# One transformer layer on one core: first feed-forward layer in 512-column matmuls, masked products of a block in one group

## The chip, the core and the metric

The kernel runs on one core of a Trainium2 chip. The metric is the device time of one execution in microseconds (us). TensorE (PE) multiplies matrices and writes to PSUM, which has eight banks of 512 float32 values a partition; VectorE (DVE) and ScalarE (ACT) read PSUM and do elementwise work; GpSimd (POOL) has little to do here; SyncE (SP) issues the loads.

## The reference

One layer with 256 tokens and a width of 1024:

```
h = RMSNorm(x); P = h @ W_in
mixer A: RWKV-7 recurrence, 8 heads x 64 (delta-rule state), + bonus sum(r k r_k) v
mixer B: causal attention, 8 heads x 64;   mixer C: causal pooling
x = x + (sum of sigmoid gates * branch projections) @ W_out
h2 = RMSNorm(x)
x = x + square(relu(h2 @ w_ff1)) @ w_ff2        w_ff1: 1024 x 4096
```

All is float32. The recurrence is computed in blocks of 128 tokens: masked products of two token-wise operands give small matrices, a triangular system is solved by levels, and four steps of 64 tokens carry the state.

## The kernel before

**Precision.** Each float32 factor is held as a high part and a rest: w_hi and w_lo of the weights, h_hi and h_lo of the activations, r_hi and r_lo of the feed-forward's hidden values. A product is three matmuls (`mm3`, lines 497 to 499): high by high, high by rest, rest by high, added up in PSUM.

**Pieces and slots.** The dense work is a list of 69 units (`UNITS`), one for each slot t. A slot uses two weight pieces of 512 KB, v = 2t and 2t + 1, and has four quarters p = 0 to 3; a place in the program is written (t, p). For every quarter each engine runs the dense part (`part`) and then what else is put there (`extra`): of the mixers on TensorE, and their copies on ScalarE and VectorE. SyncE loads a piece into one of three stages once VectorE has finished the piece three before (`lo_done`); ScalarE rounds it to w_hi (L900), VectorE subtracts to w_lo (L1142). The ring of split pieces has six places: ScalarE may write piece v when TensorE has used piece v - 6 (`used`). The splits run about five pieces ahead of TensorE. Engines follow their own program strictly in order, so an instruction that waits holds up what stands behind it.

**Banks.** `plan_turns` deals the banks out in the order of the program, and `room` makes TensorE wait until the bank's former content was copied out (`drained`). In the slots spoken of here banks 0 to 3 belong to the dense units and 4 to 7 go around in a ring.

**Slots 7 to 11.** At (7, 3) TensorE transposes v into two banks, 5 and 6; ScalarE copies these to zz (L961). The masked products of block c are computed in two groups g of two head pairs, each with 32 small matmuls (L626, L629) into two banks; `PROD_AT` puts the groups at (8, 0), (8, 2), (9, 0) and (9, 2). The bonus, two float32 matmuls of 512 columns from `att` (L706), stands at (8, 1); the profile lists each as two passes. VectorE masks the products (L1246) and multiplies the bonus into v (L1237). X0 (L722), transposes of the first solution, follows at (9, 1) and (10, 1); Y, the first level of the solution (L743), at (11, 0).

**Feed-forward, slots 37 to 68.** A first-layer unit ("ff1", i) computes 256 of the 4096 hidden columns, as two column tiles of 128 by 8 k, with weights as the stationary operand and h2 (256 tokens) as the moving one: 48 matmuls of 256 columns into one bank. ScalarE takes Relu out of PSUM (L1097) and squares it into r_hi (L1101); VectorE computes the square (L1428) and the rest r_lo (L1146). A second-layer unit ("ff2", i) multiplies these: 24 matmuls of 512 columns into banks 0 to 3, where they add up to the end. The order is ff1 0, ff1 1, ff2 0, ff1 2, ff2 1 and so on, so that ff2 i starts two slots after the end of ff1 i, in the case of the first and the last unit one slot after. The transposes of x for h2 (L881) stand at (36, 1) and (37, 0), their drains at L1051 and L1386.

Of the kernel before, what the change touches and what calls it, by code (L numbers as in the profile page):

```python
# [76 lines left out]
PROD_AT = {(8, 0): (0, 0), (8, 2): (0, 1), (9, 0): (1, 0), (9, 2): (1, 1)}  # L77
# [44 lines left out]
def plan_turns():  # L122


    turn, count, signalled, ring = {}, [0] * 8, [0] * 8, [4, 5, 6, 7]

    def use(name, bank=None, dense=False):
        if bank is None:
            bank = ring[0]
            ring.append(ring.pop(0))  # L130
        turn[name] = (bank, count[bank], signalled[bank])
        count[bank] += 1
        signalled[bank] += not dense

    for i in range(4):
        use(("x", i))
    for t, u in enumerate(UNITS):
        if t == S_HEAD:
            ring.insert(0, 3)
        if t == S_BR:  # L140
            ring.remove(3)
        for p in range(4):
            if p == 0:
                if u[0] == "feat":
                    use(("unit", t), FEAT_BANK[t], dense=True)
                elif u[0] == "tok" and u[2] == 0 and u[1] >= GATES_AT:
                    g = (u[1] - GATES_AT) // 512
                    for tt in range(TT):
                        use(("tok", u[1], tt), (2 * g + tt + 2) % 3, dense=tt == 1)
                elif u[0] == "tok" and u[2] == 0:  # L150
                    b = 0 if u[1] == N_RWKV else 2
                    use(("tok", u[1], 0), b + 1)
                    use(("tok", u[1], 1), b, dense=True)
                elif u[0] == "branch":
                    b = 2 * ((t - S_BR) % 2)
                    use(("unit", t, 0), b)
                    use(("unit", t, 1), b + 1, dense=True)
# [23 lines left out]
def pe_uses(t, p):  # L181
# [57 lines left out]
    if h2_place(t, p) is not None:  # L239
        out += [(("h2", 2 * h2_place(t, p) + i),) for i in range(2)]  # L240
# [3 lines left out]
def dense_ends():  # L244

    ends = {}
    for t, u in enumerate(UNITS):
# [9 lines left out]
        if u[0] == "ff1":  # L257
            ends[("ff", u[1])] = 2 * t + 2
# [6 lines left out]
def build_layer(nc: bass.Bass, x, w_in, w_up, w0, a_up, g_up, pool_w, w_branch, w_out, w_ff1, w_ff2, vecs, consts, out):  # L265
    turn = plan_turns()
    ctx = ExitStack()
    with ctx:
# [10 lines left out]
        h_hi = sb("h_hi", [P, KD, T], F32R)  # L279
        h_lo = sb("h_lo", [P, KD, T], F32R)  # L280
# [146 lines left out]
        f_hi, f_ready = sem("f_hi"), sem("f_ready")  # L427
# [67 lines left out]
        def _(pe):  # L495
# [37 lines left out]
            def part(t, p):  # L533
# [6 lines left out]
                if u[0] in ("feat", "ff1"):  # L540
                    name = ("unit", t) if u[0] == "feat" else ("ff", u[1])
# [5 lines left out]
                    for kk in range(4):  # L547
                        k = 4 * (p // 2) + kk
                        if k % 2 == 0 and u == ("ff1", 0) and i == 0:
                            copied(pe, ("h2", k // 2))  # L550
# [90 lines left out]
            def extra(t, p):  # L641
# [60 lines left out]
                if (t, p) == (8, 1):  # L702
# [12 lines left out]
                if (t, p) in PROD_AT:  # L715
                    products(*PROD_AT[t, p])
# [177 lines left out]
        def _(act):  # L894
# [22 lines left out]
            def extra(t, p):  # L917
# [128 lines left out]
                if h2_place(t, p) is not None:  # L1046
                    for i in (2 * h2_place(t, p), 2 * h2_place(t, p) + 1):
# [4 lines left out]
                        ins.then_inc(h2_hi, 1)  # L1052
                if (t, p) == (S_FF, 1):
# [7 lines left out]
            def finish(t):  # L1061
# [30 lines left out]
                elif u[0] == "ff1":  # L1092
                    i = u[1]
                    if i >= 2:
                        act.wait_ge(f_ready, i - 1)
                    o = take(act, ("ff", i))
                    nc.scalar.activation(ffs[i % 2], o[:], ACT.Relu).then_inc(drained_of(("ff", i)), 1)  # L1097
                    copied(act, ("ff", i))
                    if i >= 2:
                        act.wait_ge(used, 2 * (UNITS.index(("ff2", i - 2)) + 1))  # L1100
                    nc.scalar.activation(r_hi[:, 2 * (i % 2):2 * (i % 2) + 2], ffs[i % 2].rearrange("p (k t) -> p k t", k=2),  # L1101
                                         ACT.Square).then_inc(f_hi, 1)
# [27 lines left out]
        def _(dve):  # L1130
# [49 lines left out]
            def extra(t, p):  # L1180
# [51 lines left out]
                if (t, p) == (8, 1):  # L1232
# [6 lines left out]
                if (t, p) in PROD_AT:  # L1239
                    c, g = PROD_AT[t, p]  # L1240
                    if g == 0:
                        dve.wait_ge(mask_in, 16)
                    for e in range(2):
# [136 lines left out]
                if h2_place(t, p) is not None:  # L1380
                    for i in (2 * h2_place(t, p), 2 * h2_place(t, p) + 1):
# [6 lines left out]
                        ins.then_inc(drained_of(("h2", i)), 1)  # L1388
                if (t, p) == (S_FF, 3):
# [4 lines left out]
            def finish(t):  # L1394
# [30 lines left out]
                elif u[0] == "ff1":  # L1425
                    i = u[1]
                    copied(dve, ("ff", i))
                    link(dve.tensor_tensor(fsq[i % 2], ffs[i % 2], ffs[i % 2], ALU.mult))  # L1428
                    dve.wait_ge(f_hi, i + 1)
                    b = 2 * (i % 2)  # L1430
                    rest(r_lo[:, b:b + 2], fsq[i % 2].rearrange("p (k t) -> p k t", k=2), r_hi[:, b:b + 2])\
                        .then_inc(f_ready, 1)
# [139 lines left out]
```

## Time and profile before

| | us |
|---|---|
| median of 3 runs | 467.64 (467.38 to 467.68) |
| the profiled execution | 467.01 |
| span of its instructions | 465.2 |
| TensorE busy | 459.6 (99%) |
| VectorE, ScalarE busy | 295.0 (63%), 245.8 (53%) |
| granted TensorE clock, mean | 1.00 |

Busy time of TensorE counts the whole time of pipelined matmuls, which overlap: a matmul of 512 columns is listed with 0.39 us and the next one starts 0.23 us after it. So the distance between starts tells its pace, and a gap in busy time shows only part of a wait.

### The profile page before, as it was taken

The page shows a single profiled execution, that of the slowest core. Times are in us where ns is not written, and L with a number is a line of the kernel's source. Part 1 is how long each engine was busy: PE and PEld are TensorE (multiplying, and loading weights), DVE is VectorE, ACT ScalarE, POOL GpSimd, SP SyncE. Part 2 cuts the span into 40 slices and gives each one's busy share as a digit, 9 for nine tenths or more (in the row PEclk, how much of TensorE's full clock was granted, in tenths as well). Part 3 has the DMA queues.
Part 4 walks back from the last instruction along what each step waited for, and adds up shares of the span by engine and source line. Part 5 has one row for each costly group of instructions (what it writes and reads, how often), then busy time and mean ns, then how long its engine had stood idle before and what let it go on. Part 6 is the DMA issues. An engine that isn't in the chain of part 4 may idle for free.

```text
span 465.2 us, 8736 instructions
## 1 busy us (share of the span) xinstructions
PE 459.6 (99%) x3660; PEld 397.7 (85%) x3660; DVE 295.0 (63%) x405; ACT 245.8 (53%) x370; POOL 33.1 (7%) x41
## 2 busy tenths in 40 slices
PE   8999999999999999999999999999999999999997
PEld 4999986788977778788888889999999999999995
DVE  4675998674564766766778758655555555555542
ACT  5597655646555456566543538444444444444430
POOL 2000100021670001002000000000000000000000
PEclk9999999999999999999999999999999999999999
DMA  7776635533424435445656564655556656565602
GB/s 235 235 231 217 220 96 177 151 122 93 145 87 136 118 110 142 130 159 171 189 185 184 175 193 143 209 184 184 184 189 194 197 184 182 185 182 190 204 10 90
DMA packets 48694, 76.91 MB, mean 165 GB/s; under 512 B 2576, under 2 KB 28944, under 8 KB 48656
## 3 DMA queue, kind: packets, MB, share of 16 engines
q1 hardware_dynamic: 48656, 76.36, 53.1%
q8 instruction: 29, 0.48, 0.4%
q14 instruction: 9, 0.07, 0.0%
HBM read 75.30 MB, written 1.05 MB: 164 GB/s over the span
## 4 chain that ended last, share of the span: by engine, by line
PE 90%; DVE 3%; ACT 2%; DMA 2%; issue 1%; POOL 1%; DVEq 0%; ACTq 0%
PE bank L497 26%; PE bank L498 25%; PE bank L499 25%; DMA stage<-in_w_in 2%; PE bank L606 1%; PE bank L762 1%; PE bank L743 1%; DVE w_lo L1142 1%; PE bank L638 1%; ACT w_hi L900 1%; POOL small L1472 1%; DVE xs L1458 1%; PE bank L626 1%; PE bank L829 1%; PE bank L793 1%
## 5 line engine op out<-in xcount | busy, mean ns | idle before, releaser
L1142 DVE TENSOR_TENSOR w_lo<-stage,w_hi 128x1024 fp32r<-128x1024 f32 x138 | 167.9, 1225 | 89.1 <-ACT w_hi L900 89.1
L900 ACT CAST w_hi<-stage 128x1024 fp32r<-128x1024 f32 x138 | 144.5, 1052 | 109.5 <-PE bank L499 88.6
L497 PE MATMUL bank<-h_hi,w_hi 128*128 128x256 f32 x384 | 109.8, 286 | 0.3 <-DVE h_lo L1386 0.3
L498 PE MATMUL bank<-h_lo,w_hi 128*128 128x256 f32 x384 | 108.6, 283 | 0.0
L499 PE MATMUL bank<-h_hi,w_lo 128*128 128x256 f32 x384 | 108.6, 283 | 0.0
L497 PEld LDWEIGHTS bank<-h_hi,w_hi 128*128 128x128 f32 x384 | 73.6, 192 | 1.6 <-issue 0.8
L498 PEld LDWEIGHTS bank<-h_lo,w_hi 128*128 128x128 f32 x384 | 73.6, 192 | 0.6
L499 PEld LDWEIGHTS bank<-h_hi,w_lo 128*128 128x128 f32 x384 | 73.6, 192 | 0.0
L497 PE MATMUL bank<-w_hi,h_hi 128*128 128x512 f32 x144 | 60.4, 420 | 0.0
L497 PE MATMUL bank<-w_hi,r_hi 128*128 128x512 f32 x144 | 56.4, 392 | 0.0
L499 PE MATMUL bank<-w_hi,h_lo 128*128 128x512 f32 x144 | 56.4, 391 | 0.0
L498 PE MATMUL bank<-w_lo,h_hi 128*128 128x512 f32 x144 | 56.4, 391 | 0.0
L498 PE MATMUL bank<-w_lo,r_hi 128*128 128x512 f32 x144 | 56.2, 390 | 0.0
L499 PE MATMUL bank<-w_hi,r_lo 128*128 128x512 f32 x144 | 56.0, 389 | 0.0
L497 PEld LDWEIGHTS bank<-w_hi,h_hi 128*128 128x128 f32 x144 | 27.0, 188 | 7.7 <-issue 2.4
L499 PEld LDWEIGHTS bank<-w_hi,h_lo 128*128 128x128 f32 x144 | 27.0, 188 | 6.1
L499 PEld LDWEIGHTS bank<-w_hi,r_lo 128*128 128x128 f32 x144 | 27.0, 188 | 5.8
L497 PEld LDWEIGHTS bank<-w_hi,r_hi 128*128 128x128 f32 x144 | 27.1, 188 | 5.2
L498 PEld LDWEIGHTS bank<-w_lo,r_hi 128*128 128x128 f32 x144 | 27.1, 188 | 4.9
L498 PEld LDWEIGHTS bank<-w_lo,h_hi 128*128 128x128 f32 x144 | 27.1, 188 | 4.7 <-issue 0.2
L1472 POOL TENSOR_TENSOR small<-small 128x8 f32<-128x8 f32 (+2 forms) x9 | 15.0, 1676 | 173.7 <-DVE small L1320 69.1
L1097 ACT ACTIVATE mat<-bank 128x512 f32<-128x512 f32 x16 | 9.6, 599 | 30.5 <-PE bank L499 30.5
(231 smaller groups left out, 541.9 us busy)
## 6 DMA issues: line engine op xcount, KB each, us to landing
stage<-in_w_ff SPq DMA_DIRECT2D x64, 512.0 KB, 3.8
stage<-in_w_in SPq DMA_DIRECT2D x54, 512.0 KB, 3.8
stage<-in_w_branch SPq DMA_DIRECT2D x12, 512.0 KB, 4.5
stage<-in_w_out SPq DMA_DIRECT2D x8, 512.0 KB, 4.1
xs<-in_x SPq DMA_DIRECT2D x2, 512.0 KB, 3.9
out<-xs SPq DMA_DIRECT2D x4, 256.0 KB, 2.1
cst<-in_consts SPq DMA_DIRECT2D x1, 608.0 KB, 6.6
att<-in_w SPq DMA_DIRECT2D x1, 256.0 KB, 5.9
```

The source lines that it names most:

```text
L497: pe.matmul(o, lh, rh, start=first, stop=False)
L498: pe.matmul(o, lh, rl, start=False, stop=False)
L499: return pe.matmul(o, ll, rh, start=False, stop=last)
L606: pe.matmul(banks[3][:], flat[:, 0:P], flat[:, 0:512], start=True, stop=True)
L626: ins = pe.matmul(o[halves[e], P * i:P * i + P], bk[c][halves[e], j, s, 0:HD], ar[c][halves[e], j, :, HD * s:HD * s + HD], start=True, sto ...
L638: ins = pe.transpose(o[:, P * j:P * j + P], x_c[:, c, j].rearrange("p s n -> p (s n)"), ident)
L743: ins = pe.matmul(both[e][halves[s], HD * i:HD * i + HD], gm[c][halves[e], j, s, e, 0:HD], x_c[halves[e], c, j, s], start=True, stop=True)
L762: ins = pe.matmul(both[s][halves[e], HD * i:HD * i + HD], left, right, start=True, stop=True)
L900: nc.scalar.copy(w_hi[:, v % RING], stage[:, v % STAGES]).then_inc(hi_done, 1)
L1097: nc.scalar.activation(ffs[i % 2], o[:], ACT.Relu).then_inc(drained_of(("ff", i)), 1)
L1142: dve.tensor_tensor(w_lo[:, v % RING], stage[:, v % STAGES], w_hi[:, v % RING].bitcast(F32), ALU.subtract)\
L1472: pool.tensor_tensor(ap, ap, half.to_broadcast(shape), ALU.pow).then_inc(done, 1)
```

## The change

In the first feed-forward layer h_hi and h_lo now lie in one tensor, `h_two` (128 x 2 x 8 x 256). High by high and high by rest have the same stationary weights, and are one matmul of 512 columns: its first 256 results are w_hi x h_hi, the others w_hi x h_lo. The third, w_lo x h_hi, has 256 columns and is added to the second half. A column tile so fills a bank of its own, and VectorE adds the two halves of it (a reduction) into `ffs`, computes max(x, 0) * x in one instruction, and ScalarE rounds this to r_hi in the next slot; the rest follows there on VectorE. The half units have banks 6 and 7, and 4 and 5, in turn; the h2 transposes 4 and 5.

The four product groups become two, at (8, 0) and (9, 0), each over four banks. The bonus moves from (8, 1) to (10, 0).

```diff
-PROD_AT = {(8, 0): (0, 0), (8, 2): (0, 1), (9, 0): (1, 0), (9, 2): (1, 1)}
+PROD_AT = {(8, 0): 0, (9, 0): 1}
+BONUS_AT = (10, 0)
...
-                    use(("ff", u[1]), dense=True)
+                    for j in range(2):
+                        use(("ff", u[1], j), 6 - 2 * (u[1] % 2) + j, dense=j == 1)
...
-        out += [(("prod", *PROD_AT[t, p], e),) for e in range(2)]
+        out += [(("prod", PROD_AT[t, p], g, e),) for g in range(2) for e in range(2)]
...
-        out += [(("h2", 2 * h2_place(t, p) + i),) for i in range(2)]
+        out += [(("h2", 2 * h2_place(t, p) + i), 4 + i) for i in range(2)]
...
-        h_hi = sb("h_hi", [P, KD, T], F32R)
-        h_lo = sb("h_lo", [P, KD, T], F32R)
+        h_two = sb("h_two", [P, 2, KD, T], F32R)
+        h_hi, h_lo = h_two[:, 0], h_two[:, 1]
...
+                if u[0] == "ff1":
+                    name = ("ff", u[1], i)
+                    o = room(pe, name) if p < 2 else ps(name)
+                    cols = slice(P * i, P * i + P)
+                    for kk in range(4):
+                        k = 4 * (p // 2) + kk
+                        if k % 2 == 0 and u == ("ff1", 0) and i == 0:
+                            copied(pe, ("h2", k // 2))
+                        pe.matmul(o[:].rearrange("p (s t) -> p s t", s=2), wh[:, kk, cols], h_two[:, :, k],
+                                  start=k == 0, stop=False)
+                        ins = pe.matmul(o[:, T:2 * T], wl[:, kk, cols], h_hi[:, k], start=False, stop=k == KD - 1)
+                    if p == 2:
+                        ins.then_inc(full_of(name), 1)
...
-                if (t, p) == (8, 1):
+                if (t, p) == BONUS_AT:
                     pe.wait_ge(rk_ready, 1)
...
                 if (t, p) in PROD_AT:
-                    products(*PROD_AT[t, p])
+                    for g in range(2):
+                        products(PROD_AT[t, p], g)
...
+                if p == 0 and UNITS[t - 1][0] == "ff1":
+                    i = UNITS[t - 1][1]
+                    act.wait_ge(sq_ready, i + 1)
+                    if i >= 2:
+                        act.wait_ge(used, 2 * (UNITS.index(("ff2", i - 2)) + 1))
+                    nc.scalar.copy(r_hi[:, 2 * (i % 2):2 * (i % 2) + 2], fsq[i % 2].rearrange("p (k t) -> p k t", k=2))\
+                      .then_inc(f_hi, 1)
...
-                    nc.scalar.activation(ffs[i % 2], o[:], ACT.Relu).then_inc(drained_of(("ff", i)), 1)
...
-                    nc.scalar.activation(r_hi[:, 2 * (i % 2):2 * (i % 2) + 2], ffs[i % 2].rearrange("p (k t) -> p k t", k=2),
-                                         ACT.Square).then_inc(f_hi, 1)
...
+                if p == 1 and UNITS[t - 1][0] == "ff1":
+                    i = UNITS[t - 1][1]
+                    b = 2 * (i % 2)
+                    dve.wait_ge(f_hi, i + 1)
+                    rest(r_lo[:, b:b + 2], fsq[i % 2].rearrange("p (k t) -> p k t", k=2), r_hi[:, b:b + 2])\
+                        .then_inc(f_ready, 1)
...
-                    link(dve.tensor_tensor(fsq[i % 2], ffs[i % 2], ffs[i % 2], ALU.mult))
...
+                    for j in range(2):
+                        o = take(dve, ("ff", i, j))
+                        dve.tensor_reduce(ffs[i % 2][:, T * j:T * j + T], o[:].rearrange("p (s t) -> p t s", s=2), AX_X, ALU.add)\
+                           .then_inc(drained_of(("ff", i, j)), 1)
+                    for j in range(2):
+                        copied(dve, ("ff", i, j))
+                    dve.scalar_tensor_tensor(out=fsq[i % 2], in0=ffs[i % 2], scalar=0.0, in1=ffs[i % 2],
+                                             op0=ALU.max, op1=ALU.mult).then_inc(sq_ready, 1)
```

What this does to the order of the instructions, at three places. TensorE of the kernel before, from the middle of the first product group in slot 8 to the bonus (L626 and L629 are products, L706 the bonus, the others dense):

```order
L626 MATMUL bank<-ops 64x128 x2
L629 MATMUL bank<-ops 64x128 x2
L497 MATMUL bank<-w_hi,h_hi 128x512
L498 MATMUL bank<-w_lo,h_hi 128x512
L499 MATMUL bank<-w_hi,h_lo 128x512
L497 MATMUL bank<-w_hi,h_hi 128x512
L498 MATMUL bank<-w_lo,h_hi 128x512
L499 MATMUL bank<-w_hi,h_lo 128x512
L706 MATMUL bank<-att,cst 128x512 x2
```

The same place in the changed kernel, with bank numbers and waits (L639 and L642 are the products); here the first half of the group ends and the second begins:

```order
L639 MATMUL bank7<-ops 64x128
L639 MATMUL bank4<-ops 64x128
L642 MATMUL bank7<-ops 64x128
L642 MATMUL bank4<-ops 64x128
L639 MATMUL bank5<-ops 64x128 [waits drained6,drained5]
L639 MATMUL bank6<-ops 64x128
L642 MATMUL bank5<-ops 64x128
L642 MATMUL bank6<-ops 64x128
```

The second half stands right behind the first, without the dense matmuls and the bonus between, and waits for the banks of the transposed v. The bonus, on TensorE of the changed kernel in slot 10 (L743 are transposes of the operands, L719 is the bonus):

```order
L743 MATMUL bank<-cst,ops 128x128 x8
L499 MATMUL bank<-w_hi,h_two 128x512
L500 MATMUL bank<-w_lo,h_two 128x512
L501 MATMUL bank<-w_hi,h_two 128x512
L499 MATMUL bank<-w_hi,h_two 128x512
L500 MATMUL bank<-w_lo,h_two 128x512
L501 MATMUL bank<-w_hi,h_two 128x512
L719 MATMUL bank<-att,cst 128x512 x2
```

It now stands two slots later, behind all product groups. VectorE late in the feed-forward stage, before (one pair of units: L1142 splits weights, L1428 is the square, L1146 the rest):

```order
L1142 TENSOR_TENSOR w_lo<-stage,w_hi 128x1024 [waits hi_done] x4
L1428 TENSOR_TENSOR mat<-mat 128x512 [waits drained7]
L1146 TENSOR_TENSOR r_lo<-mat,r_hi 128x512 [waits f_hi,own]
L1142 TENSOR_TENSOR w_lo<-stage,w_hi 128x1024 [waits hi_done] x4
L1428 TENSOR_TENSOR mat<-mat 128x512 [waits drained4]
```

And in the changed kernel (L1444 is the reduction, L1448 relu and square, L1156 the rest, L1152 the split):

```order
L1444 TENSOR_REDUCE mat<-bank 128x256 [waits full6]
L1444 TENSOR_REDUCE mat<-bank 128x256 [waits used]
L1448 SCALAR_TENSOR_TENSOR mat<-mat 128x512 [waits drained7,drained6]
L1152 TENSOR_TENSOR w_lo<-stage,w_hi 128x1024 [waits hi_done]
L1156 TENSOR_TENSOR r_lo<-mat,r_hi 128x512 [waits f_hi]
L1152 TENSOR_TENSOR w_lo<-stage,w_hi 128x1024 [waits hi_done] x3
```

VectorE now reads PSUM itself, twice a unit, and a weight split stands between the square and the rest.

## Rows read from the trace of the kernel before

**Rows 1.** The page: busy time, the chain that ended last, loads (KB each, us to landing).
```profile
PE 459.6 (99%) x3660; PEld 397.7 (85%) x3660; DVE 295.0 (63%) x405; ACT 245.8 (53%) x370; POOL 33.1 (7%) x41
...
PE 90%; DVE 3%; ACT 2%; DMA 2%; issue 1%; POOL 1%; DVEq 0%; ACTq 0%
PE bank L497 26%; PE bank L498 25%; PE bank L499 25%; DMA stage<-in_w_in 2%; PE bank L606 1%; PE bank L762 1%; PE bank L743 1%; DVE w_lo L1142 1%; PE bank L638 1%; ACT w_hi L900 1%; POOL small L1472 1%; DVE xs L1458 1%; PE bank L626 1%; PE 
...
stage<-in_w_ff SPq DMA_DIRECT2D x64, 512.0 KB, 3.8
```
**Rows 2.** TensorE in order of time, feed-forward: start us, us, engine, line, operation.
```profile
329.74 0.39 PE L498 MATMUL bank<-w_lo,r_hi 128*128 128x512 f32 x1
...
332.91 0.28 PE L497 MATMUL bank<-h_hi,w_hi 128*128 128x256 f32 x1
...
338.66 0.40 PE L497 MATMUL bank<-w_hi,r_hi 128*128 128x512 f32 x1
```
**Rows 3.** TensorE in order of time, middle of the first first-layer unit.
```profile
284.50 0.28 PE L499 MATMUL bank<-h_hi,w_lo 128*128 128x256 f32 x1
285.07 0.36 PE L497 MATMUL bank<-h_hi,w_hi 128*128 128x256 f32 x1 [0.29 <-DVE h_lo L1386]
```
**Rows 4.** ScalarE and VectorE in order of time, after one first-layer unit's end.
```profile
327.70 0.60 ACT L1097 ACTIVATE mat<-bank 128x512 f32<-128x512 f32 x1 [1.83 <-PE bank L499]
328.33 0.63 ACT L1101 ACTIVATE r_hi<-mat 128x512 fp32r<-128x512 f32 x1
...
329.07 0.69 DVE L1146 TENSOR_TENSOR r_lo<-mat,r_hi 128x512 fp32r<-128x512 f32 x1
```
**Rows 5.** Line 1276, a reduction on VectorE: duration min/median/max in ns.
```profile
L1276 DVE TENSOR_REDUCE small<-att x4: 676/678/680, 95.3 to 114.1; 128x8 f32<-128x512 f32 x4
```
**Rows 6.** All engines in order of time, slot 8.
```profile
65.54 1.06 ACT L900 CAST w_hi<-stage 128x1024 fp32r<-128x1024 f32 x1 [4.32 <-DMA stage<-in_w_in]
...
67.01 0.33 PE L626 MATMUL bank<-ops 64*64 64x128 f32 x2
...
67.28 0.28 PE L626 MATMUL bank<-ops 64*64 64x128 f32 x2
...
67.65 1.50 ACT L961 COPY big<-bank 64x256 f32<-64x256 f32 x4
...
67.83 0.28 PE L626 MATMUL bank<-ops 64*64 64x128 f32 x2
...
68.05 0.50 PE L497 MATMUL bank<-w_hi,h_hi 128*128 128x512 f32 x1
...
69.18 1.51 ACT L961 COPY vtok<-bank 64x256 f32<-64x256 f32 x4
...
70.74 1.12 PE L706 MATMUL bank<-att,cst 128*128 128x512 f32 x2 [0.18 <-ACT vtok L961]
...
71.79 1.23 DVE L1142 TENSOR_TENSOR w_lo<-stage,w_hi 128x1024 fp32r<-128x1024 f32 x1 [1.14 <-ACT w_hi L900]
...
73.19 0.33 PE L626 MATMUL bank<-ops 64*64 64x128 f32 x2
```
**Rows 7.** TensorE in order of time, six dense matmuls and the product group after them.
```profile
80.06 0.48 PE L497 MATMUL bank<-w_hi,h_hi 128*128 128x512 f32 x1
...
81.63 0.33 PE L626 MATMUL bank<-ops,big 64*64 64x128 f32 x2
```
**Rows 8.** In order of time: VectorE's last mask step before X0, and Y's first matmul.
```profile
77.78 1.72 DVE L1261 TENSOR_TENSOR mat<-mat,cst 64x256 f32<-64x256 f32 x4
...
92.90 1.16 PE L743 MATMUL bank<-mat 64*64 64x64 f32 x64
```
**Rows 9.** First and last matmuls in order of time; then a stretch, busy us, granted clock last but two.
```profile
1.44 6.77 PE L606 MATMUL bank<-mat 128*128 128x512 f32 x8 [1.44 <-DVE mat L1148]
...
461.54 0.39 PE L499 MATMUL bank<-w_hi,r_lo 128*128 128x512 f32 x1
...
464.00:465.20 1.20, 0.00 (x0) 0.00 (x0) 0.00 (x0) 0.00 (x0) 0.00 (x0) 0.93 0.28 106
```

More of the change, by code:

```diff
@@ L257, in dense_ends @@
         if u[0] == "ff1":
-            ends[("ff", u[1])] = 2 * t + 2
+            ends[("ff", u[1], 1)] = 2 * t + 2
     return ends
@@ L426, in build_layer @@
         ss2_ready, h2_hi = sem("ss2_ready"), sem("h2_hi")
-        f_hi, f_ready = sem("f_hi"), sem("f_ready")
+        sq_ready, f_hi, f_ready = sem("sq_ready"), sem("f_hi"), sem("f_ready")
         fin_ready, stored = sem("fin_ready"), sem("stored")
@@ L539, in part @@
                 i = p % 2
-                if u[0] in ("feat", "ff1"):
-                    name = ("unit", t) if u[0] == "feat" else ("ff", u[1])
+                if u[0] == "ff1":
[11 more added lines that the diff above has]
+                        ins.then_inc(full_of(name), 1)
+                elif u[0] == "feat":
+                    name = ("unit", t)
                     if p == 0:
@@ L548, in part @@
                         k = 4 * (p // 2) + kk
-                        if k % 2 == 0 and u == ("ff1", 0) and i == 0:
-                            copied(pe, ("h2", k // 2))
                         ins = mm3(o[:, T * i:T * i + T], wh[:, kk, cols], wl[:, kk, cols], h_hi[:, k], h_lo[:, k],
@@ L701, in extra @@
                         ins.then_inc(full_of(("vt", c)), 1)
-                if (t, p) == (8, 1):
+                if (t, p) == BONUS_AT:
                     pe.wait_ge(rk_ready, 1)
@@ L1091, in finish @@
                       .then_inc(drained_of(("unit", t)), 1)
[L1092 to L1096, printed above, removed]
-                    nc.scalar.activation(ffs[i % 2], o[:], ACT.Relu).then_inc(drained_of(("ff", i)), 1)
-                    copied(act, ("ff", i))
-                    if i >= 2:
-                        act.wait_ge(used, 2 * (UNITS.index(("ff2", i - 2)) + 1))
-                    nc.scalar.activation(r_hi[:, 2 * (i % 2):2 * (i % 2) + 2], ffs[i % 2].rearrange("p (k t) -> p k t", k=2),
-                                         ACT.Square).then_inc(f_hi, 1)
             for t in range(SLOTS):
@@ L1231, in extra @@
                     ins.then_inc(rk_ready, 1)
-                if (t, p) == (8, 1):
+                if (t, p) == BONUS_AT:
                     copied(dve, ("unit", 5))
@@ L1239, in extra @@
                 if (t, p) in PROD_AT:
[L1240 to L1243, printed above, removed]
+                    c = PROD_AT[t, p]
+                    dve.wait_ge(mask_in, 16)
+                    for g, e in ((0, 0), (0, 1), (1, 0), (1, 1)):
                         name = ("prod", c, g, e)
@@ L1426, in finish @@
                     i = u[1]
-                    copied(dve, ("ff", i))
-                    link(dve.tensor_tensor(fsq[i % 2], ffs[i % 2], ffs[i % 2], ALU.mult))
[L1429 to L1432, printed above, removed]
+                    for j in range(2):
[6 more added lines that the diff above has]
+                                             op0=ALU.max, op1=ALU.mult).then_inc(sq_ready, 1)
             for t in range(SLOTS):
```

## The prediction

> **What bounds the kernel now.** I read the page first, then the order of time of the two stretches that the diff touches, then what stands on ScalarE and VectorE beside them. The page says that TensorE is busy 99% of the span and makes up 90% of the chain that ended last; the three matmul lines L497 to L499 alone are 76% of it [rows 1]. Busy time of pipelined matmuls hides short gaps, so I go by the distance between starts. In the feed-forward stretch fourteen matmuls of 512 columns start from 329.74 to 332.91, 0.226 us apart; then 48 of 256 columns (one first-layer unit) start from 332.91 to 338.66, 0.120 us apart [rows 2]. These distances don't vary and no wait stands between them, so there TensorE alone sets the pace: what it saves is saved at the end, and what it waits is lost.
>
> **First layer: fewer matmuls.** A unit is 16 triples of 256-column matmuls (two column tiles by eight k). Two of each triple use the same weights, w_hi, on h_hi and on h_lo; they become one matmul of 512 columns, and the third stays. Two of 256 take 2 x 0.1198 = 0.2396 us and one of 512 takes 3.17 / 14 = 0.2264 [rows 2]: the columns are as many, and what is left over is one matmul's fixed share, 0.0132 us. There are 16 units x 16 = 256 such pairs: 256 x 0.0132 = 3.38 us. Of this the first unit's first half gives nothing: after its 24 matmuls TensorE stands until VectorE has written the third and fourth quarter of h_lo (from 284.50 to 285.07 for a matmul that needs 0.12) [rows 3], and arriving earlier only lengthens that wait. Eight pairs, 0.11 us, are so hidden: **3.27 us saved**.
>
> No row shows a 512-column matmul whose columns lie in two runs (h_hi and h_lo, 8 KB apart), nor 512 and 256 columns in turn. Bounds: at worst the new matmul takes as long as the two it replaces (0.240, nothing saved), at best 0.226 as above. I take 0.226, since the 256-column rows already reload weights each 0.120 us, so a 256-column matmul behind a 512-column one has no less time for its load than now [rows 2]. Here the rows differ from the Trainium skill, which (TensorE: Matmul & The Clock Gate, Back-to-back issue gap) gives the gap as the columns over 2.4 GHz and about 2.5 ns. By that the pairs would save 256 x 2.5 ns = 0.6 us, less than the other half of the change costs, and the kernel would end slower; the trace does not agree, its distances leave about 13 ns over the columns at both widths.
>
> **First layer: the work behind it.** ScalarE loses its Relu (0.60) and its Square becomes a copy (0.63) a slot later; VectorE gets two reductions of 512 PSUM values to 256, and one relu-times-itself instead of a product [rows 4]. The nearest row for the reduction is 0.678 us (L1276, 512 elements) [rows 5]. Per pair of units VectorE goes from 4 x 1.23 + 2 x 0.69 = 6.3 us to 4 x 1.23 + 2 x 0.68 + 0.75 + 0.69 = 7.7, of 11.2 us in which TensorE works through two units; ScalarE falls from 5.4 to 4.8. After a unit's end the chain is reduction 0.68, product 0.75, copy 0.63, then VectorE's w_lo (1.23) in front of the rest 0.69: some 4 us, and the second layer asks for it two slots after the unit's end, for the first and the last unit one slot after it, which is 5.4 us at the least. So it costs nothing; without that cover each unit would add what it is late. What waits behind the copy on ScalarE is a w_hi split, needed five pieces later; the split ahead of it can start at the unit's end, where Relu (327.70) and Square stood before it [rows 4]. SyncE's loads wait for w_lo, which VectorE finishes at most 1.4 us later in the pair; a load asked for 2.6 us after the unit's end lands 3.8 us on [rows 1], at 6.4, before the split that wants it can start (at 8.3, when its ring place comes free). I cost it at nothing. The banks of two half units (6 and 7, then 4 and 5) come free two units ahead.
>
> **Products: two groups become one.** One group of 32 small matmuls takes from 67.01 to 68.05, 1.04 us, of which eight steps of 0.11 (five of them from 67.28 to 67.83) are 0.88 and start and drain 0.16 [rows 6]. Going from dense matmuls into such a group and back costs 0.21: six dense ones between two groups take from 80.06 to 81.63, 1.57 us, where six free ones take 6 x 0.226 = 1.36 [rows 7]. Merging saves 0.16 + 0.21 = 0.37 us where nothing has to be waited for, and so it is in slot 9: **0.37 saved**. There the four banks are those of slot 8's products, which VectorE has emptied by about 73.1, and slot 9's group comes near 77.4.
>
> **Slot 8 is different, and this is the cost.** The second half of the group needs two more banks, 5 and 6. These hold the transposed v, which ScalarE copies out at L961: first bank until 67.65 + 1.50 = 69.15, second until 69.18 + 1.51 = 70.69 [rows 6]. ScalarE is late here since it sat 4.32 us for a load, until 65.54 [rows 6]; nothing ahead of it is changed, so these times stay. Before, the bonus was the one that met this: its second matmul starts at 70.74, released by L961 [rows 6]. Now the first half ends at 67.83 + 0.11 = 67.94, TensorE stands until 70.74, and the second half takes 1.04, until 71.78. Two groups before: 2 x (1.04 + 0.21) = 2.50. Now 71.78 - 67.01 + 0.21 = 4.98: **2.48 us lost**. Behind the waiting instruction stand all matmuls of slot 8; VectorE, which now takes four products in a row, then starts w_lo of piece 21 (1.23) at about 73.1 instead of 71.79 [rows 6], and piece 21 is used two slots later.
>
> **The bonus** moves to (10, 0) and loses its wait. From 68.05 to 73.19 are 5.14 us for twelve dense matmuls (2.72), one way in and out (0.21) and the bonus, 2.21 [rows 6]. Its idle time is only shown as 0.18; its four passes at the full clock take half of what the four-and-four of L606 took at the start, 0.85 / 2 x 4 = 1.7 [rows 9], so up to 0.50 is wait. I take **0.5 saved**, with 0.18 as the other end. In slot 10 its banks (6 from the last product, 7 from X0) were emptied in slot 9, and its 1.28 us on VectorE stand ahead of two w_lo pieces that are two slots early. The mask steps for X0, which ended at 79.50 [rows 8], come behind fewer products in slot 8 and end near 78.7; X0's transposes come at about 80.8: no wait.
>
> **Sum.** -3.27 + 2.48 - 0.37 - 0.5 = -1.66 us. The profiled execution took 467.01 (span 465.2 and 1.8 around it) and would take 465.35; the median of three is 467.64, 0.63 above it, and the forecast is 467.64 - 1.66 = **466.0 us**.
>
> **Rivals.**
> 1. The 512-column matmul in two runs saves nothing (0.240). For: no row shows one, and two runs or the change of width might cost an issue. Against: the distances at both widths leave the same 13 ns. Then 467.64 + 1.61 = 469.2, slower; it decides as soon as less than 1.61 / 256 = 6.3 ns is saved a pair. By the Trainium skill's gap rule the time would be 468.6. 12%.
> 2. The clock falls. At the end the last matmul is over at 461.93, and from 464.00 to 465.20 the granted clock is 0.93 in the mean [rows 9]: a fall from 2.4 to 1.2 GHz would stand 0.17 us before the end, about 3.1 us after the last matmul. The new wait is 2.8 us. Were it to fall, and to stay low for as long as L606 ran at the start (6.8 us), half of that is lost: 466.0 + 3.4 = 469.4, slower. The Trainium skill (TensorE: Matmul & The Clock Gate, Why this matters for your kernels) warns of just such gaps between bursts; the trace agrees that one lowers the clock, at its end. 6%.
> 3. The wait in slot 8 isn't there, or small, since ScalarE comes to the copies earlier. Then the merges save 0.37 twice: 467.64 - 3.27 - 0.74 - 0.5 = 463.1. Nothing in the diff moves what ScalarE waits for. 7%.
> 4. Both halves cancel within the bound: 0.007 to 0.010 us saved a pair, or a wait for a late bank behind the bonus in slots 9 to 11, of up to 1 us. 466.7 to 468.6. 13%.
> The forecast's own mechanism, 465.2 to 466.7, has 62%.
>
> **How the numbers follow.** About 0.2% is what a measurement of this kernel can tell from no change, here 0.94 us: faster means under 466.7, slower over 468.6. Faster: forecast and rival 3, 0.69. Same: rival 4, 0.14. Slower: rivals 1 and 2, 0.17. The range takes in rival 4 and the lower part of rivals 1 and 2: 464.8 to 468.9.
>
> **What would show it.** In the changed profile: 512- and 256-column matmuls of a unit 0.226 and 0.120 apart, a unit 5.55 us long instead of 5.75; TensorE idle about 2.7 us before a product matmul near 70.7, released by the copy into vtok; no wait at the bonus near 86; Y's first matmul some 1.6 us later than 92.90 [rows 8]; full granted clock throughout. It would be wrong if the unit stays at 5.75, or if second-layer matmuls wait for r_lo.

## The result

The changed kernel is slower: 468.97 us (median of 20 runs) against 467.49 us (20 runs of the kernel before beside them), a ratio of 1.0031 with a 95% interval of 1.0018 to 1.0044. The forecast was 466.0. The profiled execution took 470.85 us with a span of 469.1, where that of the kernel before had 467.01 and 465.2.

The page of the changed kernel: span, busy times, the granted TensorE clock in forty slices (tenths of full speed), and the chain that ended last, by engine:

```profile
span 469.1 us, 8226 instructions
...
PE 459.6 (98%) x3404; PEld 386.2 (82%) x3404; DVE 311.9 (67%) x437; ACT 237.9 (51%) x354; POOL 33.0 (7%) x41
...
PEclk9999997999999999999999999999999999999999
...
PE 83%; DMA 7%; DVE 5%; ACT 3%; issue 1%; SPq 0%; DVEq 0%; ACTq 0%
```

The second line is to be set beside [rows 1]: 256 matmuls fewer, and TensorE just as long busy. The third shows one slice with less than the full clock, at some 70 to 82 us, which is slots 8 and 9. DMA has 7% of the chain where it had 2% [rows 1]: up to 66.7 us the chain now goes through loads and the splits behind them, the last of them the load for which ScalarE waited.

What happened there stands in the order of time, first ScalarE, then TensorE (to be compared with [rows 6]):

```profile
66.65 1.06 ACT L914 CAST w_hi<-stage 128x1024 fp32r<-128x1024 f32 x1 [5.61 <-DMA stage<-in_w_in]
...
68.75 1.50 ACT L975 COPY big<-bank 64x256 f32<-64x256 f32 x4
70.28 1.50 ACT L975 COPY vtok<-bank 64x256 f32<-64x256 f32 x4
```

```profile
71.92 0.48 PE L639 MATMUL bank<-ops 64*64 64x128 f32 x2 [3.48 <-ACT vtok L975]
...
73.84 0.79 PE L499 MATMUL bank<-w_hi,h_two 128*128 128x512 f32 x1
74.43 0.63 PE L500 MATMUL bank<-w_lo,h_two 128*128 128x512 f32 x1
74.86 0.63 PE L501 MATMUL bank<-w_hi,h_two 128*128 128x512 f32 x1
...
77.84 0.57 PE L499 MATMUL bank<-w_hi,h_two 128*128 128x512 f32 x1
78.25 0.40 PE L500 MATMUL bank<-w_lo,h_two 128*128 128x512 f32 x1
78.49 0.40 PE L501 MATMUL bank<-w_hi,h_two 128*128 128x512 f32 x1
```

The wait is where the prediction put it, and the copies of the transposed v release it, but it is 3.48 us of idle time. And behind it dense matmuls of 512 columns start 0.43 us apart, until 78.25, where they go back to 0.23. Stretches of the same profile, columns as in [rows 9], show why: the last but two is the granted clock.

```profile
69.00:71.00 2.00, 0.00 (x0) 0.00 (x0) 2.00 (x3) 1.93 (x6) 0.00 (x0) 1.00 0.27 29
71.00:72.00 1.00, 0.07 (x4) 0.11 (x7) 0.79 (x2) 0.95 (x4) 0.00 (x0) 0.69 0.88 272
72.00:78.00 6.00, 6.00 (x42) 4.80 (x43) 2.48 (x4) 1.90 (x2) 0.00 (x0) 0.50 0.42 130
78.00:79.00 1.00, 1.00 (x6) 0.79 (x5) 1.00 (x1) 0.08 (x1) 0.00 (x0) 0.89 0.82 291
```

A mean of 0.69 over one us is a fall from 2.4 to 1.2 GHz at 71.4, some 3 us after the last product of the first half, while TensorE was idle; 0.89 is a rise at 78.2. From 71.92 to 78.2 TensorE worked at half speed, so about 3 us of these 6.3 are lost; e5, below, gives the price more closely.

The first feed-forward layer got faster, but less than forecast. One unit in the order of time; the next line after it is the second layer:

```profile
338.00 0.39 PE L550 MATMUL bank<-h_two,w_hi 128*128 128x512 f32 x1
338.23 0.28 PE L552 MATMUL bank<-h_two,w_lo 128*128 128x256 f32 x1
338.34 0.40 PE L550 MATMUL bank<-h_two,w_hi 128*128 128x512 f32 x1
338.57 0.28 PE L552 MATMUL bank<-h_two,w_lo 128*128 128x256 f32 x1
338.69 0.40 PE L550 MATMUL bank<-h_two,w_hi 128*128 128x512 f32 x1
338.93 0.28 PE L552 MATMUL bank<-h_two,w_lo 128*128 128x256 f32 x1
339.05 0.40 PE L550 MATMUL bank<-h_two,w_hi 128*128 128x512 f32 x1
...
343.64 0.40 PE L499 MATMUL bank<-w_hi,r_hi 128*128 128x512 f32 x1
```

The unit takes 5.64 us, against 5.75 in [rows 2] and 5.55 forecast. Three wide and three narrow matmuls take 1.05 us (338.00 to 339.05), 0.35 a pair where 0.227 + 0.120 = 0.347 was expected; over all sixteen it is 0.3525.

**Where the time went, by stretches of TensorE.** From the starts of the matmuls in each trace: S1 is from the first product to the first matmul of Y, S2 from there to the first one of the feed-forward, S3 from there to the last one's start. In the changed kernel's trace S1 begins at 67.35 and ends at 98.63; 67.01 [rows 6] and 92.90 [rows 8] are its ends in that of the kernel before.

```profile
98.63 0.29 PE L757 MATMUL bank<-mat 64*64 64x64 f32 x4
```

| profiled kernel | S1 | S2 | S3 |
|---|---|---|---|
| before | 25.89 | 187.99 | 180.65 |
| changed | 31.28 | 187.99 | 178.77 |

5.39 us are lost in S1 and 1.88 won in S3. Ahead of S1 0.33 us are lost as well, in a part of the program that the change leaves alone. The sum, 3.84, is the difference of the two spans.

The twenty runs of the changed kernel fall into groups by their mean granted clock:

| mean granted clock | runs | median us |
|---|---|---|
| 1.000 | 3 | 467.13 |
| 0.996 | 11 | 468.88 |
| 0.993 | 6 | 470.80 |

A mean of 0.993 over 469 us is 6.6 us at half clock, which is the profiled execution's case, and 0.996 about half of that. The steps between the medians are 1.8 and 1.9 us. The three runs at the full clock are 0.4 us under the kernel before.

### The profile page after: what moved, and what is told of

It reads as the page before. It is cut to its first block, busy times and chain, and to the rows that moved or that the text cites. A ratio compares the mean times of both kernels' runs of the same rounds, so it can differ in the third digit from the quotient of the medians.

```text
span 469.1 us, 8226 instructions
## 1 busy us (share of the span) xinstructions
PE 459.6 (98%) x3404; PEld 386.2 (82%) x3404; DVE 311.9 (67%) x437; ACT 237.9 (51%) x354; POOL 33.0 (7%) x41
## 3 DMA queue, kind: packets, MB, share of 16 engines
HBM read 75.30 MB, written 1.05 MB: 163 GB/s over the span
## 4 chain that ended last, share of the span: by engine, by line
PE 83%; DMA 7%; DVE 5%; ACT 3%; issue 1%; SPq 0%; DVEq 0%; ACTq 0%
PE bank L499 18%; PE bank L500 17%; PE bank L501 17%; PE bank L550 13%; DMA stage<-in_w_in 7%; PE bank L552 6%; DVE w_lo L1152 2%; ACT w_hi L914 1%; PE bank L757 1%; PE bank L776 1%; PE bank L651 1%; PE bank L639 1%; DVE h_two L1174 1%; DVE xs L1475 1%; PE bank L843 1%
## 5 line engine op out<-in xcount | busy, mean ns | idle before, releaser
L1152 DVE TENSOR_TENSOR w_lo<-stage,w_hi 128x1024 fp32r<-128x1024 f32 x138 | 167.9, 1223 | 90.4 <-ACT w_hi L914 90.3
L550 PE MATMUL bank<-h_two,w_hi 128*128 128x512 f32 x256 | 91.1, 398 | 0.3 <-DVE h_two L1395 0.3
L552 PE MATMUL bank<-h_two,w_lo 128*128 128x256 f32 x256 | 71.8, 281 | 0.0
L499 PE MATMUL bank<-w_hi,h_two 128*128 128x512 f32 x144 | 61.1, 424 | 0.0
L550 PEld LDWEIGHTS bank<-h_two,w_hi 128*128 128x128 f32 x256 | 48.1, 188 | 12.2 <-issue 0.6
L500 PE MATMUL bank<-w_lo,h_two 128*128 128x512 f32 x144 | 57.1, 396 | 0.0
L501 PE MATMUL bank<-w_hi,h_two 128*128 128x512 f32 x144 | 57.1, 396 | 0.0
L552 PEld LDWEIGHTS bank<-h_two,w_lo 128*128 128x128 f32 x256 | 48.3, 189 | 0.6
L499 PE MATMUL bank<-h_two,w_hi 128*128 128x256 f32 x128 | 37.3, 292 | 0.0
L500 PE MATMUL bank<-h_two,w_hi 128*128 128x256 f32 x128 | 36.2, 283 | 0.0
L501 PE MATMUL bank<-h_two,w_lo 128*128 128x256 f32 x128 | 36.2, 283 | 0.0
L499 PEld LDWEIGHTS bank<-w_hi,h_two 128*128 128x128 f32 x144 | 27.6, 191 | 7.8 <-issue 2.2
L501 PEld LDWEIGHTS bank<-w_hi,h_two 128*128 128x128 f32 x144 | 27.5, 191 | 6.2
L500 PEld LDWEIGHTS bank<-w_lo,h_two 128*128 128x128 f32 x144 | 27.7, 192 | 5.0 <-issue 0.2
```

The costliest lines, as they stand in the source:

```text
L499: pe.matmul(o, lh, rh, start=first, stop=False)
L500: pe.matmul(o, lh, rl, start=False, stop=False)
L501: return pe.matmul(o, ll, rh, start=False, stop=last)
L550: pe.matmul(o[:].rearrange("p (s t) -> p s t", s=2), wh[:, kk, cols], h_two[:, :, k], start=k == 0, stop=False)
L552: ins = pe.matmul(o[:, T:2 * T], wl[:, kk, cols], h_hi[:, k], start=False, stop=k == KD - 1)
L1152: dve.tensor_tensor(w_lo[:, v % RING], stage[:, v % STAGES], w_hi[:, v % RING].bitcast(F32), ALU.subtract)\
```

## Experiments

Each kernel was timed in turns with the kernel before, on one chip a job. Medians of the kernel before in the three jobs: 467.42 (e1 to e4), 467.46 (e5 to e7), 467.31 (e8 to e11).

### The two halves of the change, each alone

e1: the product groups and the bonus moved, the first layer as before.

```diff
-PROD_AT = {(8, 0): (0, 0), (8, 2): (0, 1), (9, 0): (1, 0), (9, 2): (1, 1)}
+PROD_AT = {(8, 0): 0, (9, 0): 1}
+BONUS_AT = (10, 0)
...
```

> The kernel before with the product groups and the bonus moved, first layer untouched. Theory (the loss is the wait in slot 8 and the clock that falls behind it): TensorE idle 2.8 to 3.7 us before the second half of slot 8's group, and a granted clock of 0.993 to 0.996 in most executions; about 1.6 us lost where the clock stays, 3 to 5.4 us where it falls: near 470.5. Rival (the first layer is what became slower): within 0.5 us of the kernel before.

Measured: 471.42 us, ratio 1.0085 (1.0067 to 1.0102); granted clock 0.992 to 0.996 in all six runs; 3.4 us idle at the second half of the group, S1 31.01, S3 180.65. The second half starts at 71.32 after 3.44 us of idle time, so the matmuls before it were over at 67.88. Two stretches, the granted clock last but two:

```profile
67.88:70.00 2.12, 0.00 (x0) 0.00 (x0) 2.12 (x3) 2.06 (x6) 0.00 (x0) 1.00 0.05 8
70.00:71.00 1.00, 0.00 (x0) 0.00 (x0) 1.00 (x2) 0.96 (x4) 0.00 (x0) 0.65 0.79 152
```

A mean of 0.65 in the second is 0.7 us at half clock at its end: the clock fell at 70.3, 2.4 us after the last matmul.

e2: the changed kernel with products and bonus put back.

```diff
-PROD_AT = {(8, 0): 0, (9, 0): 1}
-BONUS_AT = (10, 0)
+PROD_AT = {(8, 0): (0, 0), (8, 2): (0, 1), (9, 0): (1, 0), (9, 2): (1, 1)}
+BONUS_AT = (8, 1)
...
```

> The kernel before with the first layer in 512-column matmuls, products and bonus at their old places. Theory: a first-layer unit takes 5.64 us as in the changed kernel's trace against 5.75, sixteen units give 1.8 us: 465.7, granted clock 1.00. Rival (VectorE's reductions or late r_lo cost time elsewhere): 467.5 or more.

Measured: 466.13 us, ratio 0.9972 (0.9960 to 0.9984); clock 1.000 in all seven runs; S1 26.53, S3 178.77. S3 gives the 1.88 us. The median shows 1.3 of them; in this trace the bonus waits longer for ScalarE's copies than in that of the kernel before, and S1 is 0.64 us longer, which would account for the rest.

The changed kernel once more beside them, e4:

> The changed kernel, to stand beside the others on the same chip. Both theories: about 469, granted clock mostly 0.993 to 0.996; where it is 1.00, about 467.2.

Measured: 468.88 us, ratio 1.0035 (1.0021 to 1.0048), clock 0.993 or 0.996 in all six runs. So the products cost 4.0 us alone, the first layer gives 1.3, and together they cost 1.5. These medians don't add up by 1.2 us. Among runs of one mean clock e1 is 1.8 to 2.0 us over e4 (471.87 against 470.08 at 0.993 and below, 470.60 against 468.57 at 0.995 and 0.996), which is the 1.88 of S3. The rest is the longer S1 of e2 and the number of runs with 6.6 us of half clock (three of six in e1, two of six here). The rival that VectorE's reductions cost time is out: their chain takes 0.68, 0.69, 0.63 and 0.69 us, no wait of TensorE for r_lo stands in the traces, and a second-layer unit takes 5.47 us before and after.

### What keeps the first layer from its forecast

e3: e2 with h_hi and h_lo of a k side by side, so that 512 columns are one run.

```diff
-        h_two = sb("h_two", [P, 2, KD, T], F32R)
-        h_hi, h_lo = h_two[:, 0], h_two[:, 1]
+        h_two = sb("h_two", [P, KD, 2, T], F32R)
+        h_hi, h_lo = h_two[:, :, 0], h_two[:, :, 1]
...
-                        pe.matmul(o[:].rearrange("p (s t) -> p s t", s=2), wh[:, kk, cols], h_two[:, :, k],
+                        pe.matmul(o[:].rearrange("p (s t) -> p s t", s=2), wh[:, kk, cols], h_two[:, k],
```

> As e2, but h_two is laid out so that h_hi and h_lo of one k lie side by side: the 512 columns are one run instead of two, 8 KB apart. Theory A (the second run costs the 9 ns by which the new matmul exceeds 227): starts 0.227 and 0.120 apart, a unit 5.55 us, 464.2. Theory B (the turn of widths costs them): the same as e2, a unit 5.64 us, 465.7.

Measured: 465.62 us, ratio 0.9962 (0.9950 to 0.9974), which overlaps e2. TensorE in order of time, first and last lines of one unit:

```profile
333.38 0.39 PE L550 MATMUL bank<-h_two,w_hi 128*128 128x512 f32 x1
333.61 0.28 PE L552 MATMUL bank<-h_two,w_lo 128*128 128x256 f32 x1
...
339.02 0.40 PE L499 MATMUL bank<-w_hi,r_hi 128*128 128x512 f32 x1
```

Again 5.64 us, and S3 is again 178.77. The two runs cost nothing; theory A is out.

e8: the changed kernel with early copies (e6, below), and the widths in blocks of four.

```diff
                         pe.matmul(o[:].rearrange("p (s t) -> p s t", s=2), wh[:, kk, cols], h_two[:, :, k],
                                   start=k == 0, stop=False)
+                    for kk in range(4):
+                        k = 4 * (p // 2) + kk
                         ins = pe.matmul(o[:, T:2 * T], wl[:, kk, cols], h_hi[:, k], start=False, stop=k == KD - 1)
```

> e6, but in each quarter of a first-layer unit the four 512-column matmuls come first and the four 256-column ones after them, so that the width turns twice instead of eight times. Theory B (the turn of widths costs about 7 ns a pair): four pairs take 1.39 us instead of 1.41, a unit 5.57 us instead of 5.64, in all 1.2 us less than e6: 463.9. Rival (the 512-column matmul costs 236 ns whatever is beside it): 465.1 as e6.

Measured: 464.47 us, ratio 0.9938 (0.9926 to 0.9950), against 465.05 of e6. A unit in order of time:

```profile
331.90 1.07 PE L550 MATMUL bank<-h_two,w_hi 128*128 128x512 f32 x4
332.80 0.64 PE L554 MATMUL bank<-h_two,w_lo 128*128 128x256 f32 x4
333.28 1.09 PE L550 MATMUL bank<-h_two,w_hi 128*128 128x512 f32 x4
334.21 0.63 PE L554 MATMUL bank<-h_two,w_lo 128*128 128x256 f32 x4
...
337.48 0.40 PE L499 MATMUL bank<-w_hi,r_hi 128*128 128x512 f32 x1
```

The unit falls to 5.58 us. The first four wide ones, behind wide ones of the second layer, take 0.90 (331.90 to 332.80); the next four, behind narrow ones, 0.93. So wide matmuls are slower for a while after narrow ones. The kernel before has that too, at the start of a second-layer unit, where it wasn't looked for:

```profile
338.90 0.40 PE L498 MATMUL bank<-w_lo,r_hi 128*128 128x512 f32 x1
339.13 0.39 PE L499 MATMUL bank<-w_hi,r_lo 128*128 128x512 f32 x1
339.36 0.40 PE L497 MATMUL bank<-w_hi,r_hi 128*128 128x512 f32 x1
...
340.05 0.39 PE L497 MATMUL bank<-w_hi,r_hi 128*128 128x512 f32 x1
340.28 0.39 PE L498 MATMUL bank<-w_lo,r_hi 128*128 128x512 f32 x1
```

The four from 338.66 [rows 2] to 339.59 take 0.93, later ones 0.227 each, that is 0.91. Theory B holds in kind. In size it doesn't: later first-layer units are 0.05 us shorter, but a second-layer unit behind the new order is 0.02 us longer, the first two first-layer units together are 0.3 us longer, and S3 is 178.57, only 0.18 under e6, where 1.2 was expected. What the turn does inside TensorE, and whether wide matmuls in still longer blocks would give back all of the missing 1.4 us, stays open. The 0.6 us between the medians of e8 and e6 come from different jobs and are not shown to be this; the intervals of the two ratios overlap.

### The wait and the clock

e6: the changed kernel, in slot 7 of ScalarE's program the copies ahead of the second weight split.

```diff
+                if t == 7:
+                    extra(t, 2)
+                    extra(t, 3)
                 for v in () if late else split_places(2 * t + 1):
                     high(v)
...
-                if t != 3:
+                if t not in (3, 7):
                     extra(t, 2)
                 finish(t)
-                extra(t, 3)
+                if t != 7:
+                    extra(t, 3)
```

> The changed kernel, but in slot 7 ScalarE makes the copies of the transposed v before the weight split that sits waiting for a load. Theory: both banks are empty about 3 us earlier, TensorE waits under 1 us in slot 8, granted clock 1.00: 465.3. Rival (the split that is now later is missed, or the wait comes from elsewhere): 467 or more.

Measured: 465.05 us, ratio 0.9950 (0.9936 to 0.9965), 3.9 us under the changed kernel. Eleven of twelve runs have a clock of 0.999 or 1.000; the twelfth has 0.996 and 467.94. The kernel before has 0.996 too in 3 of its 58 runs in the three jobs, so now and then the clock falls without the long wait; no trace shows where. ScalarE in order of time, and TensorE at the second half of the group:

```profile
65.02 1.50 ACT L975 COPY big<-bank 64x256 f32<-64x256 f32 x4 [3.06 <-PE bank L713]
66.55 1.50 ACT L975 COPY vtok<-bank 64x256 f32<-64x256 f32 x4
68.07 1.99 ACT L914 CAST w_hi<-stage 128x1024 fp32r<-128x1024 f32 x2
```

```profile
68.19 0.33 PE L639 MATMUL bank<-ops 64*64 64x128 f32 x2 [0.35 <-ACT vtok L975]
```

The idle time is 0.35 us instead of 3.48, and TensorE has no wait for the split that now comes later. S1 falls to 25.83.

e7 is e6 with h_hi and h_lo side by side.

> e6 with h_hi and h_lo of a k side by side. If the second run costs 9 ns a matmul: 463.5 to 463.8, faster than all the others. If not: as e6.

Measured: 465.20 us, ratio 0.9955 (0.9943 to 0.9967): as e6, and the second answer that the two runs cost nothing.

e5 separates the fall of the clock from the wait. Twelve matmuls whose results nobody reads are put between the two halves; they need nothing that isn't there, and the halves wait for the banks as before.

```diff
+FILL = 12
...
                     for g in range(2):
+                        if (t, g) == (8, 1):
+                            for _ in range(FILL):
+                                pe.matmul(banks[1][:].rearrange("p (s t) -> p s t", s=2), h_hi[:, 0, 0:P], h_hi[:, 0:2],
+                                          start=True, stop=True)
                         products(PROD_AT[t, p], g)
```

> The changed kernel with 12 matmuls of 512 columns put between the two halves of slot 8's group, into a bank that nobody reads then: TensorE works for 2.7 us of its wait. Theory (the fall of the clock is a price of its own, on top of the wait): granted clock 1.00 in all executions, the wait for the banks as long as before, 467.5 and so about 1.5 us under the changed kernel. Rival (the wait is all, the clock says little): as the changed kernel, 469, or more for the added work.

Measured: 467.84 us, ratio 1.0008 (0.9996 to 1.0020); clock 0.999 or 1.000 in eleven of twelve runs, and 0.996 in the one at 469.46. The second half is released by the same copies as before, now after 0.20 us of idle time. From the first product it starts 4.27 us on, where it was 4.57 in the changed kernel's trace:

```profile
71.15 0.33 PE L640 MATMUL bank<-ops 64*64 64x128 f32 x2 [0.20 <-ACT vtok L980]
```

S1 is 28.07 against 31.28, and 0.30 of these 3.21 us are the shorter wait. What follows the wait is the same work in both: from the start of the second half to Y's first matmul it takes 26.71 us in the changed kernel (71.92 to 98.63) and 23.81 here (71.15 to 94.96).

```profile
94.96 0.29 PE L762 MATMUL bank<-mat 64*64 64x64 f32 x4
```

So 2.9 us are the price of the clock in the profiled execution, apart from the wait. In the medians the kernel with more work is faster by 1.1 us; the two come from different jobs and their intervals just touch (0.9996 to 1.0020 against 1.0018 to 1.0044), so it is the clock of the single runs that shows the effect.

e10: the same with `FILL = 4`.

> e5 with 4 instead of 12 added matmuls: TensorE is idle for about 2.6 us at a stretch instead of 3.5 (changed kernel) or 0.2 (e5), about the wait that the prediction counted on. If a wait of that length leaves the clock alone: granted clock 1.00, 467.8 as e5. If not: clock 0.993 to 0.996 in part of the executions, and those at 469 to 471.

Measured: 468.64 us, ratio 1.0010 (0.9991 to 1.0029). The runs fall in two: five with 0.999 or 1.000, 466.49 to 466.90; seven with 0.996, 468.60 to 470.14 (median 469.11). The profiled one is of the second kind. The end of its idle time, then stretches, with the granted clock last but two:

```profile
71.41 0.33 PE L640 MATMUL bank<-ops 64*64 64x128 f32 x2 [2.31 <-ACT vtok L980]
```

```profile
69.00:71.40 2.40, 0.10 (x1) 0.02 (x1) 2.32 (x3) 2.31 (x7) 0.00 (x0) 1.00 0.52 125
71.40:74.00 2.60, 2.59 (x34) 2.11 (x35) 0.89 (x2) 0.94 (x1) 0.00 (x0) 0.58 0.78 284
74.00:77.00 3.00, 3.00 (x12) 2.44 (x11) 1.70 (x3) 1.05 (x1) 0.00 (x0) 0.80 0.18 23
```

TensorE was idle for 2.3 us only. By starts, as the prediction counted its 2.8 us, the gap is 2.6: the added matmuls start from 67.90, 0.227 apart, and so the last one's turn ends at 68.81. The clock was full to 71.40, and a mean of 0.58 over the next 2.6 us is 2.2 us at half speed: it fell at about 71.8, when TensorE had been working again for 0.4 us. So a gap a little shorter than the predicted one was followed by a fall. In this trace the fall costs 1.5 us: from the second half's start to Y's first matmul are 25.35 us, against 23.81 in e5. The two kinds of runs are 2.5 us apart (469.11 against 466.58), more than that, and the five at the full clock are 1.3 us under the median of e5, which was timed in another job. Their waits were probably shorter, as the load on which the wait hangs may have landed earlier; that is not shown, since the idle time is known for the profiled execution alone.

### What the merges and the bonus are worth without the wait

e9: e6 with product groups and bonus at their old places (diff as in e2).

> e6 with product groups and bonus at the places of the kernel before: the first layer changed, the copies early. Theory (merging two groups saves 0.37 us where nothing is waited for, and early copies take the bonus's wait of 0.5 us away): 465.8 to 466.0, that is 0.5 us over e6. Rival (the merges are worth nothing): as e6, 465.1.

Measured: 466.09 us, ratio 0.9967 (0.9954 to 0.9979), 1.0 over e6. The traces don't bear that out: S1 is 25.79, in e6 25.83, and the profiled execution of e9 was 0.94 us later already at the first product (67.69 against 66.74), ahead of which the two programs are the same. So in the traces the merges are worth nothing in sum, and the inconclusive 1.0 us of the medians (the intervals overlap) I leave aside. The bonus waits in neither of the two, so what was forecast to show here are two merges of 0.37 us. The rows of e6 show where this 0.74 went. Part goes into what is left of the wait (above): the group of slot 8 takes 2.48 us, that of slot 9, without a wait, 1.91. The rest goes into a wait at X0, which TensorE now reaches before the masks are done; the six dense matmuls and the wait ahead of it take 2.07 us here, 1.79 in e9, and 1.51 in the changed kernel:

```profile
78.87 0.63 PE L736 MATMUL bank<-cst,mat 128*128 128x128 f32 x4 [0.39 <-DVE mat L1259]
```

e11: the kernel before with the early copies alone (diff as in e6).

> The kernel before, with the copies of the transposed v ahead of the weight split in slot 7 and nothing else. Theory: the bonus's wait of 0.2 to 0.5 us goes: 467.0 to 467.2. Rival (the split that is now later delays something): 467.5 or more.

Measured: 466.73 us, ratio 0.9989 (0.9980 to 0.9998): the bonus's wait is gone, 0.6 us in the median, 0.13 in S1 (25.76). By starts the bonus takes 1.31 us instead of 1.76, from its first pass to the next dense matmul; 0.3 of the 0.45 come back at X0, as in e9.

| kernel | us | ratio to before | S1 | S3 |
|---|---|---|---|---|
| e1 products only | 471.42 | 1.0085 | 31.01 | 180.65 |
| changed | 468.97 | 1.0031 | 31.28 | 178.77 |
| e4 changed, again | 468.88 | 1.0035 | 31.09 | 178.89 |
| e10 fill 4 | 468.64 | 1.0010 | 29.89 | 178.93 |
| e5 fill 12 | 467.84 | 1.0008 | 28.07 | 178.93 |
| e11 copies first only | 466.73 | 0.9989 | 25.76 | 180.65 |
| e2 first layer only | 466.13 | 0.9972 | 26.53 | 178.77 |
| e9 copies first, old places | 466.09 | 0.9967 | 25.79 | 178.93 |
| e3 e2, one run | 465.62 | 0.9962 | 26.66 | 178.77 |
| e7 e6, one run | 465.20 | 0.9955 | 25.83 | 178.89 |
| e6 changed, copies first | 465.05 | 0.9950 | 25.83 | 178.75 |
| e8 e6, fewer turns | 464.47 | 0.9938 | 25.81 | 178.57 |

## Why the prediction was wrong

The direction was wrong, the places were right: the wait in slot 8 with its releaser, and the gain of the first layer. Without the fall of the clock the changed kernel is about level with the kernel before: its three runs at the full clock have a median 0.4 us under it, and e5, which keeps the clock and the wait, is 0.4 over it. That it is not 1.7 under even then is due to two mis-sized terms, the wait and the first layer. Step by step:

**The clock was the step that failed.** It was a rival with 6%, and the sum charged nothing. It came in 17 of 20 runs. In the profiled execution it cost 2.9 us. What spoke against it was that the clock fell 3.1 us after the last matmul in [rows 9] and that 2.8 us is less. One row from one end of one execution shows when it fell that time, not the shortest idle time behind which it falls: in e1 it fell 2.4 us after the last matmul, and in e10 behind 2.3 us of idle time. With e5 the clock stays and most of the loss is gone. The rival's price, half of 6.8 us, was near. The prediction named the Trainium skill's warning (TensorE: Matmul & The Clock Gate, Why this matters for your kernels). The section states it for gaps of more than about 3 us, and the 3.48 us of the changed kernel agree with it; the gap of 2.3 us in e10 is below that, and there the measurement decides.

**The wait in slot 8** was put at 2.48 us net. Its mechanism was right, its length depends on when a load lands that ScalarE waits for: its split starts at 65.54 in [rows 6], and at 66.65 in the changed kernel, though the program ahead of it is the same. In e1 to e5 and e10 it starts between 65.71 and 66.66. The trace of the kernel before was the earliest of eight, and the sentence that these times stay was wrong. Against the first product, which moves too, the split starts 1.47 us ahead in that trace and 0.69 to 1.00 us ahead in the seven others: the wait was read from the luckiest of them. The halves stand 3.74 us apart in the changed kernel's trace instead of 2.91, which makes the term 3.3 us.

**The first layer** was put at 3.27 us and gave 1.88. The mis-sized term is the wide matmul: 0.226 was read from the steady middle of a second-layer unit, and taken for matmuls that follow a narrow one each time. The sentence that a load has no less time than now was an argument about loads, and no row stood behind it; the bound from above (0.240) was the better half of it. Of rival 1, which would have cost everything, 40% came true, by one of its two mechanisms: two runs of columns cost nothing (e3, e7), the turn of widths does (e8). The Trainium skill's gap rule (TensorE: Matmul & The Clock Gate, Back-to-back issue gap) would have made it 0.6 us, an estimate; the measured 1.88 lies between that and the forecast, and the rule has no turn of widths.

**Merges and bonus** were put at 0.87 us, and in the changed kernel they gave 0.84. From the first product of slot 9 to the eight transposes at the end of that slot are 7.00 us before and 6.61 after: 0.39 for the merge, forecast 0.37. The bonus takes 1.31 us instead of 1.76 from its first pass to the next dense matmul: 0.45, forecast 0.5. Its four passes stand together in the changed kernel.

```profile
90.41 1.88 PE L719 MATMUL bank<-att,cst 128*128 128x512 f32 x4
```

S1 of the changed kernel is 25.89 + 3.3 (wait) + 2.9 (clock) - 0.84 = 31.25 by these terms, and measured 31.28. Without the long wait (e6 against e9) the merges don't show, because short waits take their place.

**VectorE, ScalarE and the loads** at nothing: right. The reduction took 0.683 us where 0.678 was taken from [rows 5], and S3 shows no wait of TensorE but the one at the first unit, which was foreseen [rows 3].

**The sum** with what was measured: -1.88 + 3.3 + 2.9 - 0.84 = +3.5 us for the profiled execution, and with the 0.33 us ahead of S1 3.8, against 3.84 (470.85 - 467.01). Over all twenty runs the clock costs less, and the median is 1.5 us over the kernel before.

The change as such was worth having: with ScalarE's copies moved forward it is 2.4 us faster than the kernel before (e6). With fewer turns it was 2.8 us (e8), which is not shown to be more than e6.

## What to carry to other kernels

On a TensorE that is always busy, a wait of two to three us can cost more than its length, as the clock may fall with it: before a group is moved forward, ask when its banks are emptied, and move the copies that empty them too. The time at which a transfer lands moves by a us between executions (1.1 us over eight traces here), so a wait that hangs on it has a range, and one trace gives one draw from it. Take a matmul's pace from rows with the same neighbours, since the middle of a uniform stretch is the best case.

## What the hardware did that I had not expected

- In e10's trace the granted clock fell behind 2.3 us of idle time, about 0.4 us after TensorE had begun to work again; the clock is low in 7 of that kernel's 12 runs, and in 17 of 20 of the changed kernel, whose trace has 3.5 us of idle time. In e1 it fell 2.4 us after the last matmul. It stayed low for 3.4 us in e10's trace (0.58 and 0.80 in the stretches above) and for 6.8 us in the changed kernel's.
- Twelve useless matmuls in the wait kept the clock up, in 11 of 12 runs, and took 2.9 us out of the work behind it; in the medians the kernel was faster by 1.1 us (467.84 against 468.97).
- After 256-column matmuls, 512-column ones start 0.93 us per four instead of 0.91, and in strict turns a pair takes 0.3525 us instead of 0.347, whether the columns lie in one run or in two (e2, e3).
